# Expert values: 26 of 64 pairs of units by seven block products, with sums of weights on GpSimd

## The reference

```
q = (h @ w_query) ...; scores by sub_keys; top 16 of 128 x 128 candidates, 8 heads
g = softmax(top_s)
act = gelu(einsum('td,tkd->tk', x, expert_u[idx]))
out = einsum('tk,tkd->td', g * act, expert_v[idx])
return rms_norm(x + out, norm_final)
```

## Time and profile before

| what | value |
|---|---|
| median of 3 runs | 1962.53 us (1961.2 to 1962.88) |
| the profiled execution's own time | 1965.11 us |
| its span | 1963.3 us |
| PE busy | 1901.9 us, 97% |
| DVE busy | 1397.2 us, 71% |
| ACT busy | 1145.7 us, 58% |
| POOL busy | 403.0 us, 21% |
| mean granted clock of PE | 0.991 |

### The profile page before, as it was taken

The page is one execution under the profiler, slowest core; times in us unless marked ns, Lnnn a source line. Parts: engine busy times, 40 slices in busy tenths (PEclk is TensorE's granted clock), DMA queues, the critical chain, the costliest instruction groups (busy, mean ns, idle before and its releaser), DMA issues. The chain is left out here.

```text
span 1963.3 us, 34673 instructions
## 1 busy us (share of the span) xinstructions
PE 1901.9 (97%) x14088; PEld 1771.1 (90%) x14088; DVE 1397.2 (71%) x2526; ACT 1145.7 (58%) x1943; POOL 403.0 (21%) x395
## 2 busy tenths in 40 slices
PE   8999999899999789999999999999999999999997
PEld 5798999898888789999899999999999998888886
DVE  6787776877777687557856578999987755555554
ACT  4865544556777455445755554477777754444544
POOL 0010011002332200012101200068859920000000
PEclk9999999999999899999999999999999999999999
DMA  9465787346453557666444455554454455555553
GB/s 362 169 203 184 253 279 263 127 151 191 154 168 121 184 172 232 187 187 230 140 151 151 149 164 179 187 162 151 151 162 140 143 167 186 191 185 191 188 187 118
DMA packets 97742, 356.23 MB, mean 181 GB/s; under 512 B 11104, under 2 KB 11232, under 8 KB 97200
## 3 DMA queue, kind: packets, MB, share of 16 engines
q1 hardware_dynamic: 84240, 305.04, 47.4%
q0 software_dynamic: 12624, 48.08, 7.7%
q10 hardware_dynamic: 720, 0.91, 0.1%
HBM read 352.94 MB, written 1.05 MB: 180 GB/s over the span
## 5 line engine op out<-in xcount | busy, mean ns | idle before, releaser
L2180 DVE TENSOR_TENSOR wl<-raw,wh 128x1024 fp32r<-128x1024 f32 (+1 forms) x566 | 693.8, 1230 | 369.4 <-ACT wh L1475 368.0
L1475 ACT ACTIVATE wh<-raw 128x1024 fp32r<-128x1024 f32 (+1 forms) x566 | 593.6, 1050 | 413.4 <-PE psum L602 368.3
L600 PE MATMUL psum<-peer_hh,wh 128*128 128x256 f32 x1024 | 295.6, 289 | 0.0
L602 PE MATMUL psum<-peer_hh,wl 128*128 128x256 f32 x1024 | 290.4, 284 | 0.0
L601 PE MATMUL psum<-peer_hl,wh 128*128 128x256 f32 x1024 | 290.4, 284 | 0.0
L601 PE MATMUL psum<-wl,csh 128*128 128x512 f32 x512 | 202.0, 394 | 0.0
L600 PE MATMUL psum<-wh,csh 128*128 128x512 f32 x512 | 201.8, 394 | 0.0
L602 PE MATMUL psum<-wh,csl 128*128 128x512 f32 x512 | 201.8, 394 | 0.0
L600 PEld LDWEIGHTS psum<-peer_hh,wh 128*128 128x128 f32 x1024 | 194.4, 190 | 0.0
L601 PEld LDWEIGHTS psum<-peer_hl,wh 128*128 128x128 f32 x1024 | 194.3, 190 | 0.0
L602 PEld LDWEIGHTS psum<-peer_hh,wl 128*128 128x128 f32 x1024 | 194.2, 190 | 0.0
(11 more groups left out here) (478 smaller groups left out, 4823.6 us busy)
## 6 DMA issues: line engine op xcount, KB each, us to landing
raw<-in_mlp_w SPq DMA_DIRECT2D x128, 512.0 KB, 4.2
raw<-in_eu SPq DMA_DIRECT2D x128, 512.0 KB, 3.4
raw<-in_ev SPq DMA_DIRECT2D x128, 512.0 KB, 3.3
araw<-in_ada_w POOLq DMA_DIRECT2D x76, 512.0 KB, 4.5
raw<-in_dil_qk SPq DMA_DIRECT2D x48, 512.0 KB, 4.2
raw<-in_dil_v SPq DMA_DIRECT2D x24, 512.0 KB, 3.5
raw<-in_w_in SPq DMA_DIRECT2D x16, 512.0 KB, 3.4
raw<-in_w_query SPq DMA_DIRECT2D x16, 512.0 KB, 3.5
```

The source lines that it names most:

```text
L600: e.matmul(o, l[0], r[0], start=start, stop=False, skip_group_check=loose)
L602: i = e.matmul(o, l[1], r[0], start=False, stop=stop, skip_group_check=loose)
L1475: e.activation(b.wh[v % NSPLIT][:, 0:cols], b.raw[v % NRAW][:, 0:cols], ACT.Copy).then_inc(S.hi, 1)
L2180: e.tensor_tensor(b.wl[v % NSPLIT][:, 0:cols], b.raw[v % NRAW][:, 0:cols], b.wh[v % NSPLIT][:, 0:cols].bitcast(F32), ALU.subtract).then_in ...
```

## The change

Two units of expert values and their coefficients form a 2 x 2 block product: tokens in two halves, two units of experts, features in two halves. It needs eight block products, or seven with sums of operands (the scheme of Winograd). The change does this for 26 pairs: (16, 17), (20, 21), ..., (116, 117) (`SEVEN`). Between two such pairs two ordinary units are computed. The order of PE's work is `EV`: in each group of four units `b11` (one block, 3 products), `b2` (two blocks, 6), two ordinary units `n` (12 each), `t12` (6) and `t34` (6). Four more banks (`"seven"`) collect what is common to several results over all 26 pairs, and are added to the output once at the end (`m.U`).

GpSimd makes the sums: `S1` to `S4` of the coefficients (128 columns each, into `m.S`) and `T1` to `T4` of the weights (512 columns each, into `b.xT`, whose contents PE has read by then). `m.S` is split into `m.Sp` (one pair) by ScalarE (mark `"S hi"`) and VectorE (`"S lo"`), in their programs just ahead of the split of `b2`. T1 and T2 are split as a unit `t12`, T3 and T4 as `t34`. There are now five pairs for splits (`m.slots`) and six for coefficients. The load four places on also waits for the sums that read its buffer.

At the end the last three units are computed first for tokens 0 to 127, then for tokens 128 to 255, and squares, root and scaling are done for each half by itself. In the dilated mixer's end `scores` (7, 1) moves behind the unit `dil_w_o` 0, the probabilities and `turn` (7, 0) behind their scores, and one tick from before unit 0 to behind unit 5.

```diff
--- before.py
+++ after.py
@@ -275,7 +275,7 @@
         for g in {1: (0,), 2: (1, 2)}.get(z, ()):
             if c:
                 out.append(("root square", c - 1, g))
-        if z in (0, 2) or z == 4 and c in (0, 8):
+        if z in (0, 2) or z == 4 and c == 0 or z in (4, 5) and c == 8:
             out.append(("tick", c, z))
         if c and z in (1, 2, 3):
             out.append(("scale", c - 1, z - 1))
@@ -287,13 +287,11 @@
     for z in range(6):
         out.append(late[z])
         beside(8, z)
-    out += [("tick", 8, 6), ("tick", 8, 7)]
-    tail = [[("pv", 6, 0), ("pv", 6, 1), ("scores", 7, 0), ("scores", 7, 1), ("out", 6, 0)],
-            [("probs", 7, 0), ("probs", 7, 1)], [("turn", 7, 0)], [("turn", 7, 1), ("pv", 7, 0)],
-            [("pv", 7, 1), ("out", 7, 0)], [], [], []]
+    tail = [[("pv", 6, 0), ("pv", 6, 1), ("scores", 7, 0), ("out", 6, 0)], [("scores", 7, 1), ("probs", 7, 0)],
+            [("probs", 7, 1), ("turn", 7, 0)], [("turn", 7, 1), ("pv", 7, 0)], [("pv", 7, 1), ("out", 7, 0)], [], [], []]
     for i, steps in enumerate(tail):
         out += steps + [("dil_w_o", i, 0)]
-        out += [("tick", 9, i)] * (0, 1, 2, 2, 2, 1, 0, 0)[i]
+        out += [("tick", 9, i)] * (0, 1, 2, 2, 2, 2, 0, 0)[i]
     return out
 
 
@@ -334,6 +332,47 @@
 PLAN = plan()
 UNIT_OF = {(name, blk): u for u, (name, blk, _) in enumerate(PLAN)}
 AHEAD = NSPLIT - 1
+EV0 = UNIT_OF["ev", 0]
+SEVEN = range(16, 118, 4)
+
+
+def ev_order():
+
+    out = [("n", i) for i in range(16)]
+    for i in SEVEN:
+        out += [("b11", i), ("b2", i + 1), ("n", i + 2), ("n", i + 3), ("t12", i), ("t34", i)]
+    return out + [("n", i) for i in range(120, 128)]
+
+
+EV = ev_order()
+EV_AT = {key: v for v, key in enumerate(EV)}
+EV_FIVE = 14
+EV_RING = [(EV0 + EV_FIVE + z) % NSPLIT for z in range(NSPLIT)] + [3, 4]
+EV_SLOT = [(EV0 + v) % NSPLIT if v < EV_FIVE else EV_RING[(v - EV_FIVE) % 5] for v in range(len(EV))]
+EV_PREV = [max([w for w in range(v) if EV_SLOT[w] == EV_SLOT[v]], default=None) for v in range(len(EV))]
+
+
+def ev_split(i):
+
+    return EV_AT[("n", i) if ("n", i) in EV_AT else ("b2", i) if i % 2 else ("b11", i)]
+
+
+def ev_last(i):
+
+    return EV_AT[("n", i) if ("n", i) in EV_AT else ("t34", i - 1) if i % 2 else ("b11", i)]
...
@@ -508,6 +547,9 @@
 
     m = b.peer = Bufs()
     s = ExitStack()
+    with ExitStack() as t:
+        fifth = pair("slot", UNIT, t)
+        m.S, m.Sp = sb("sums", 512, where=t), pair("sums", 512, t)
     m.C = sb("C", 128 * 256, where=s)
     m.C3 = m.C.rearrange("p (i t) -> p i t", i=128)
     tail = [m.C[:, (64 + 8 * z) * 256:] for z in range(8)]
...
@@ -539,7 +581,13 @@
         with ExitStack() as tt:
             far = [pair("cs", 256, tt) for _ in range(2)]
             m.nf = sb("nf", 1024, where=tt)
-    m.cs = near + far
+            fourth = pair("slot", UNIT, tt)
+    m.cs = near[0:2] + far + near[2:4]
+    m.slots = [[h, l] for h, l in zip(b.wh, b.wl)]
+    m.slots += [fourth, fifth]
+    m.xt = m.C[:, 8192:10240].rearrange("p (t n) -> p t n", t=2)
+    m.U = [m.C[:, z:z + 512] for z in range(10240, 12800, 512)]
+    m.fsq = m.C[:, 12800:13312]
     m.one = []
     for slot in range(2):
         o = m.C3[:, 96 + 8 * slot:104 + 8 * slot, 128:256]
...
-                       False, loose=True)
-        for i in range(128):
-            j = weights("ev", i)
+                       False, loose=True, mark=("ev init",))
+        seven = {}
+
+        def coefficients(i, t):
             pe.wait_ge(S.dve, at["coef", i])
-            for t in range(2):
+            return sp(m.cs[i % 6], 0, 256, t * 128, 128)
+
+        def sums(i, z):
+            pe.wait_ge(S.dve, at["S lo", i])
+            return sp(m.Sp, z, 128)
+
+        def product(o, x, w, first=False, last=False):
+            e.matmul(o, x[0], w[0], start=first, stop=False, skip_group_check=True)
+            e.matmul(o, x[0], w[1], start=False, stop=False, skip_group_check=True)
+            return e.matmul(o, x[1], w[0], start=False, stop=last, skip_group_check=True)
+
+        for v, (kind, i) in enumerate(EV[:-NSPLIT]):
+            pe.wait_ge(S.lo, EV0 + v + 1)
+            left, right = [sp(m.slots[EV_SLOT[v]], 0, 1024, z, 512) for z in (0, 512)]
+            first, last = i == SEVEN[0], i == SEVEN[-1]
+            if kind == "n":
+                for t in range(2):
+                    x = coefficients(i, t)
+                    product(acc[t][0], x, left)
+                    done = product(acc[t][1], x, right)
+            elif kind == "b11":
+                if first:
+                    seven = {z: take("seven", z) for z in (1, 5, 6, 7)}
+                done = product(seven[1], coefficients(i, 0), left, first, last)
+            elif kind == "b2":
+                product(acc[0][0], coefficients(i, 0), left)
+                done = product(acc[0][1], sums(i - 1, 3), right)
+            elif kind == "t12":
+                product(seven[5], sums(i, 0), left, first, last)
+                done = product(seven[6], sums(i, 1), right, first, last)
+            else:
+                product(seven[7], sums(i, 2), left, first, last)
+                done = product(acc[1][0], coefficients(i + 1, 1), right)
+            done.then_inc(S.unit, 1)
+        for t in range(2):
+            for v in range(len(EV) - NSPLIT, len(EV)):
+                i = EV[v][1]
+                pe.wait_ge(S.lo, EV0 + v + 1)
+                x = coefficients(i, t)
                 for h in range(2):
-                    mm3(acc[t][h], sp(m.cs[i % 4], 0, 256, t * 128, 128), wsp(j, h * 512, 512), False, i == 127,
-                        unit=t == 1 and h == 1, loose=True)
+                    done = product(acc[t][h], x, sp(m.slots[EV_SLOT[v]], 0, 1024, h * 512, 512), False, i == 127)
+                if t == 1:
+                    done.then_inc(S.unit, 1)
+                elif i == 127:
+                    done.then_inc(S.pe, 1)
+                    n[0] += 1
+                    at["ev", "first tokens"] = n[0]
 
     mla()
     mlp(0, "n1")
@@ -2096,29 +2188,51 @@
                 ac.wait_ge(S.pe, at["one", "mm", i])
                 act(m.C3[:, x:128, 4 * i:4 * i + 4], bank("one", i).rearrange("p (t i) -> p i t", t=4)[:, x:128, :],
                     ACT.Copy, mark=("gather", "act", i))
-        for i in range(128):
-            unit("ev", i)
-            for k in range(2 if i == 0 else 0):
-                coef_high(k)
-            if i + 2 < 128:
-                coef_high(i + 2)
-        xt = m.C[:, 0:2048].rearrange("p (t n) -> p t n", t=2)
-        ac.wait_ge(S.unit, len(PLAN))
+        for v, (kind, i) in enumerate(EV):
+            if kind not in ("t12", "t34"):
+                coef_high(i)
+            if kind == "b2":
+                ac.wait_ge(S.pool, at["S", i - 1])
+                if i - 1 > SEVEN[0]:
+                    ac.wait_ge(S.unit, EV0 + EV_AT["t34", i - 5] + 1)
+                act(m.Sp[0], m.S, ACT.Copy, mark=("S hi", i - 1))
+            if v >= AHEAD:
+                ev_high(v, kind, i)
+            if (kind, i) == ("n", 123):
+                ac.wait_ge(S.unit, EV0 + EV_AT["t34", SEVEN[-1]] + 1)
+                act(m.U[0], bank("seven", 1), ACT.Copy, mark=("seven", 1))
         for t in range(2):
             for h in range(2):
                 ac.wait_ge(S.act, n[0])
-                act(m.C[:, 2048:2560], bank("acc", t, h), ACT.Square, scale=1.0 / 32,
-                    accum_out=m.fs[:, 2 * t + h:2 * t + h + 1], mark=("final square",))
-        ac.wait_ge(S.dve, at["final sum"])
-        act(m.gs[:, 0:2], m.fs[:, 4:6], ACT.Sqrt, bias=eps, mark=("final sqrt",))
+                ac.wait_ge(S.dve, at["final add", t, h])
+                act(m.fsq, m.xt[:, t, h * 512:h * 512 + 512], ACT.Square, scale=1.0 / 32,
+                    accum_out=m.fs[:, 2 * t + h:2 * t + h + 1], mark=("final square", t))
+            ac.wait_ge(S.dve, at["final sum", t])
+            act(m.gs[:, t:t + 1], m.fs[:, 4 + t:5 + t], ACT.Sqrt, bias=eps, mark=("final sqrt", t))
+
+    def ev_high(v, kind, i):
+        src = ev_source(b, kind, i)
+        if kind in ("t12", "t34"):
+            ac.wait_ge(S.pool, at["T", kind, i])
+        else:
+            u = EV0 + i
+            ac.wait_ge(S.raw[u % NRAW], 16 * (u // NRAW + 1))
+        if EV_PREV[v] is None:
+            ac.wait_ge(S.unit, EV0 + min(0, v - NSPLIT + 1))
+            if EV_SLOT[v] == 4:
+                ac.wait_ge(S.dve, at["coef", 7])
+        else:
+            ac.wait_ge(S.unit, EV0 + EV_PREV[v] + 1)
+        high, low = ev_pair(b, v, 512 if kind == "b11" else 1024)
+        e.activation(high, src, ACT.Copy).then_inc(S.hi, 1)
 
     def coef_high(i):
         m = b.peer
         ac.wait_ge(S.dve, at["gather", "dve", 63])
         ac.wait_ge(S.dve, at["eu", "out", i // 2])
         if i >= 2:
-            ac.wait_ge(S.unit, UNIT_OF["ev", 0] + max(0, i - 3))
-        act(m.cs[i % 4][0], m.C3[:, i, :], ACT.Copy, mark=("coef hi", i))
```

(100 more changed lines are left out.)

## The result

Before 1962.41 us (the table ahead has three of its four runs), after 2032.04 us (median of 4 runs, 2028.24 to 2034.42): ratio 1.0349, 95% interval 1.0332 to 1.0367: slower by 3.5%. The forecast was 2047 (2000 to 2082), slower. The profiled execution of after took 2029.94 us, 1.8 more than its span.

What follows compares the result with a forecast made beforehand. PE alone was taken to bound the expert values. Span 1963.3 - 7 (dilated end) - 0.7 (group 16) + 94 (wait with contention) - 2.1 (end) = 2047.5; device 2047 us, own range 2030 to 2062, full range 2000 to 2082.

Steps and rivals of the forecast that it cites:

- The sign and the mechanism: Expert values: slower, chance 0.93; S hi waits for t34 of the group before, delaying b2's split and PE.
- chain from b11 to b2: Each group: S hi, b2's high part, its low part, then PE starts b2 3.35 us after b11, idle 2.65.
- The wait's term: Expert groups: period 13.38 us against 11.17, 2.21 more in 25 groups, 55 us, without contention.
- the clock falls in every group: Rival: PE's idle time in each group halves its clock; 0.8 us more each, 20 us, 2067 us; chance 0.15.
- The contention's term: Expert groups: GpSimd's sums and VectorE's splits wait for each other; period 14.93 us, total cost 94 us instead of 55.
- hand schedule: One expert group with contention: last T sum ends near 2.9 us, b2's low part 4.1, PE starts b2 at 4.25.
- second pause: PE's idle time between b2 and the next unit: 0.25 us without contention, 0.9 with S sums in VectorE's way.
- wait alone: Rival: expert groups pay the wait without contention, 55 us instead of 94; 2008 us; chance 0.25.
- shared ports are the bound: Rival: VectorE and GpSimd never overlap in expert groups; period 16.2 us, 125 us more, 2078 us; chance 0.12.
- One reading of the rows: Expert units before: VectorE's splits beside GpSimd TensorScalars average 1.23 us, so those do no such harm.
- The dilated end: Dilated mixer's end: new order brings `dil_w_o` 0 to 653.9 and `dil_w_o` 6 to 684 to 686; gain 7 us, 0 to 9.
- The end: Last product to span's end: halves done beside PE, second half's adds behind first half's scalings; gain 2.1 us, 0 to 3.

Runs made afterwards that it cites:

- run without sums: Changed kernel with GpSimd's sums left out, m.S filled once with a constant, so the output is not the reference's: 2013.28 us.
- second pair of tiles: Changed kernel with two pairs of tiles m.Sp in turn, so S hi waits for t34 of the group before last: 2018.3 us.
- doubled dose: Kernel before plus unused GpSimd two-input subtractions beside its expert units, eight of 512 and eight of 128 columns, 26 times: 2144.29 us.
- one-input dose: Kernel before plus eight unused GpSimd TensorScalars a group, each reading one SBUF tile, beside its expert units: 2050.84 us.
- wait and sums gone: Changed kernel with two pairs of tiles for the sums' split and GpSimd's sums left out, output not the reference's: 1933.88 us.
- two kernels whose PE never waits: Changed kernel with two pairs of tiles and no GpSimd sums, 1933.88 us; changed kernel with a group every eight units, 1944.20 us.

## Why the prediction was right, and where its sum was off

**The sign and the mechanism** held: one pair of tiles for the sums' split, ScalarE in order, b2's split queued behind it, PE waiting for VectorE before one product in each group. Its chain from b11 to b2, forecast 3.35 us, came out as 3.09 in the run without sums. What made it shorter is to be seen there: the b2 high part began at 1749.68, 0.09 before the sums' high part had ended (1749.14 + 0.63), and PE starts 0.06 after its split (1750.75 + 1.23), not 0.15.

**The wait's term.** Forecast 55 us (2.21 x 25). In the run without sums the mean period was 13.60: (13.60 - 11.17) x 25 = 61, of which (13.02 - 11.17) x 25 = 46 without the clock and 15 by it. The rival *the clock falls in every group* was right in part: a fall costs 1.4 us there, and comes in 10 of 25 groups; in after it comes in 7 of 25 and adds 0.20 x 25 = 5. That the forecast's 55 lies between 46 and 61 is in part luck: the chain was put too long, and the clock at nothing.

**The contention's term was mis-sized.** The forecast added 39 us for it (94 - 55). On top of the wait it was (13.94 - 13.02) x 25 = 23 where the clock did not fall, and in all 14.5 by the stages (431.2 - 416.7; 19 by the two times, 2032.0 - 2013.3), since the clock fell more rarely in after. PE's wait in front of b2 was 2.4 to 2.7 us where 3.5 was forecast, and the period 14.14 where it was 14.93. Two steps of the hand schedule were too late: the last T sum was put at 2.9 after b11's start and ended at 1.76, so that b2's low part ended at 3.44 and not at 4.1; and the S sums cost 0.50 more in the second pause, not 0.65. In all the stage grew by 74; the forecast has 93 (94 less 0.7 for the first group). The forecast's 2047 is 15 us above the 2032 measured, the rival *wait alone*, 2008, 24 below.

**Why the two are not a sum** the prediction did not see. It asked what the contention adds to the wait and never what it would cost without the wait: 84 us. So it would have promised 55 for a second pair of tiles, and the chip gave 14. The rival *shared ports are the bound* had this limit, but at 16.2 us a group (9.2 + 7.0); measured is 13.66. In the doubled dose 16 instructions in turn take 11.35 us (48 products x 200 / 846) of 13.8 alone: by this estimate some 0.15 us of each of the 16 goes on beside the other engine.

**One reading of the rows** was wider than its words: the earlier trace rows are not of the 200 us of the earlier trace rows but of 1500 us to the end, and most of their splits had no TensorScalar beside them. The conclusion stands all the same. Over the whole kernel before, 76 of these splits had one beside them and took 1.25 us in the mean, against 1.22 for those with GpSimd idle; and the run with the one-input dose shows it at full load.

**Nothing behind them.** The loads, ScalarE's 8.1 us and the five sums of the banks were costed at nothing; PE busy 200 of 200 us with wait and sums gone bears that out.

**The dilated end**: forecast -7 (0 to 9), measured -9.0 in after at the next MLP and -7.7 at the first product of the expert values; there it was between -6.9 and -10.3 in the other runs with this order, -9.3 in the run of it alone. `dil_w_o` 0 starts at 653.69 (forecast 653.9), `dil_w_o` 6 at 684.70 (684 to 686), 7.5 earlier than the earlier trace rows. The probabilities began at 660.91 (661.3). The last 1.5 us: before, the clock stood at 0.50 behind the second wait, while in after it was 1.00 from 684 to 690, when units 6 and 7 ran.

**The end**: forecast -2.1, measured -1.5. The second half's adds do stand behind the first half's scalings:

```profile
2019.09 1.42 DVE L2274 SCALAR_TENSOR_TENSOR C<-C,gs,nf 128x512 f32<-128x512 f32 x2
...
2020.61 1.29 DVE L2266 TENSOR_TENSOR C<-psum,C 128x512 f32<-128x512 f32 x2
...
2023.62 1.42 DVE L2274 SCALAR_TENSOR_TENSOR C<-C,gs,nf 128x512 f32<-128x512 f32 x2
```

They end at 2020.51, 1.87 after the last product's start at 2018.64, not 1.5.

## What to carry to other kernels

Work taken off the bound engine pays only if its new pace leaves room for what the saving adds elsewhere: here 0.70 us of products a group cost a new wait and a VectorE slowed by GpSimd, and at half the density (13 groups instead of 26) the same code gained. Cost each new limit by itself, as a period, and take the largest as the least that it will be (here 13.66 us by the turns alone, 13.94 in after); a cost found on top of another says nothing about what is left when the other is gone. A single buffer between two in-order engines needs work between its last reader and its next use: 3 products here gave a wait of 2.4 us, 51 (four plain units and b11) gave none.

## What was not expected of the hardware

- VectorE and GpSimd take turns, instruction by instruction (141 and 142 in 200 us with GpSimd's queue never empty). Doubling GpSimd's work did not slow VectorE further.
- Only GpSimd's two-input instructions got in VectorE's way: TensorScalars that read one SBUF tile filled 190 of 200 us and the splits stayed at 1.226 and 0.420 us. The Trainium skill (SBUF — State Buffer, Who interferes with whom) says that a two-input VectorE instruction contends with any GpSimd instruction that reads SBUF; the sums agree with it (1.79 us), the TensorScalars here don't.
- PE's granted clock fell to 0.50 in 10 of 25 groups with one idle stretch of 2.24 us (no sums), in 7 of 25 with 2.4 to 2.7 and a second of 0.3 (after), and in none with 2.3 to 2.4 and 0.34 (two pairs of tiles, period 13.66). A longer idle stretch alone does not decide it. What does stays open.
- In the two kernels whose PE never waits, a product takes 0.2316 us in the mean (337.40 / 1457 and 346.38 / 1496), before 0.2327: 1.6 us over the stage beyond the products saved. The trace shows which ones: those that read a unit's split in the two new pairs (`sloth`, `slotl`) follow each other in 0.229 us, those that read `wh`, `wl` in 0.233 as before. What sets these tiles apart was not tested.
